# A row scale moved from the activations to the products, in two matmul stages of a transformer-block kernel

## The reference, cut to what matters

```
# first block's feed-forward (w_up is 1024 x 5632, 44 chunks of 128 outputs)
h = rmsnorm(x, norm_ffn_g) @ w_up          # rmsnorm: x * rsqrt(mean(x*x)) * g
h = causal_conv3(h, conv_w) + conv_b       # per channel, over tokens
a, b = split(h);  x = x + (silu(a) * b) @ w_down

# last layer's feed-forward (w1 is 1024 x 4096, 32 chunks)
h = rms(x, g) * (1 + scale) + shift
x = x + gate * square(relu(h @ w1)) @ w2
```

## Time and profile before

| | us |
|---|---|
| median of 3 runs | 1424.33 (1420.19 to 1426.97) |
| the profiled execution | 1423.98 |
| its span in the trace | 1422.2 |
| PE busy | 1366.4 (96%), 8436 matmuls |
| DVE busy | 714.1 (50%) |
| ACT busy | 604.7 (43%) |
| POOL busy | 448.6 (32%) |
| mean granted TensorE clock | 0.989 |

### The profile page before, as it was taken

How to read it: one execution, slowest core, us unless ns; L and a number is a source line. 1 busy time by engine, 2 the same in 40 slices (tenths; PEclk the granted TensorE clock), 3 DMA queues, 4 the chain that set the end, 5 groups by cost and what they waited for, 6 DMA issues and landing times.

```text
span 1422.2 us, 20872 instructions
## 1 busy us (share of the span) xinstructions
PE 1366.4 (96%) x8436; PEld 1158.2 (81%) x8436; DVE 714.1 (50%) x1129; ACT 604.7 (43%) x997; POOL 448.6 (32%) x440
## 2 busy tenths in 40 slices
PE   7889999999999999998999999999899999899999
PEld 7777788789999677875788888888577777799999
DVE  7575447757765635227122232222657766844443
ACT  6334445556664322225332133322445544665432
POOL 4532121333342000314440024401266643477200
PEclk9999999999999999999999999999999999999999
DMA  7346567686555445245533332323522221455552
GB/s 279 118 167 206 194 228 242 216 299 234 178 178 179 180 166 173 87 137 184 172 100 93 100 100 93 103 90 104 207 97 96 79 101 45 163 166 187 182 182 85
DMA packets 63968, 220.14 MB, mean 155 GB/s; under 512 B 6912, under 2 KB 10240, under 8 KB 63872
## 3 DMA queue, kind: packets, MB, share of 16 engines
q1 hardware_dynamic: 63584, 218.56, 46.2%
q10 hardware_dynamic: 288, 0.25, 0.1%
HBM read 217.73 MB, written 1.05 MB: 154 GB/s over the span
## 4 chain that ended last, share of the span: by engine, by line
PE 80%; DVE 9%; POOL 4%; ACT 3%; issue 2%; DMA 1%; SPq 0%; DVEq 0%; POOLq 0%; ACTq 0%
PE ps L476 23%; PE ps L490 22%; PE ps L488 22%; PE ps L532 3%; DVE wlo L1419 2%; PE ps L795 1%; POOL tmp L2144 1%; PE ps L822 1%; PE ps L742 1%; PE ps L809 1%; DVE tmp L1685 1%; DVE tmp L1687 1%; DVE Alo L1832 1%; PE ps L483 1%; PE ps L788 1%
## 5 line engine op out<-in xcount | busy, mean ns | idle before, releaser
L476 PE MATMUL ps<-Ahi,whi 128*128 128x256 f32 (+1 forms) x1656 | 552.6, 334 | 16.6 <-ACT Ahi L942 7.0
L490 PE MATMUL ps<-Ahi,wlo 128*128 128x256 f32 (+1 forms) x1584 | 509.2, 321 | 2.2 <-DVE wlo L1419 2.2
L488 PE MATMUL ps<-Alo,whi 128*128 128x256 f32 (+1 forms) x1584 | 509.4, 322 | 0.7 <-DVE Alo L1433 0.5
L1419 DVE TENSOR_TENSOR wlo<-raw,whi 128x1024 fp32r<-128x1024 f32 x298 | 373.3, 1261 | 226.6 <-ACT whi L913 226.5
L913 ACT ACTIVATE whi<-raw 128x1024 fp32r<-128x1024 f32 x305 | 320.2, 1052 | 263.9 <-PE ps L490 217.5
L476 PEld LDWEIGHTS ps<-Ahi,whi 128*128 128x128 f32 x1656 | 319.4, 193 | 93.8 <-issue 40.8
L490 PEld LDWEIGHTS ps<-Ahi,wlo 128*128 128x128 f32 x1584 | 305.2, 193 | 24.8 <-DVE wlo L1419 3.3
L488 PEld LDWEIGHTS ps<-Alo,whi 128*128 128x128 f32 x1584 | 305.4, 193 | 23.6 <-issue 1.9
L488 PE MATMUL ps<-Hlo,whi 128*128 128x256 f32 (+2 forms) x752 | 240.0, 319 | 0.4 <-DVE Hlo L1433 0.4
L476 PE MATMUL ps<-Hhi,whi 128*128 128x256 f32 (+2 forms) x712 | 229.0, 322 | 0.0
L490 PE MATMUL ps<-Hhi,wlo 128*128 128x256 f32 (+2 forms) x712 | 228.6, 321 | 0.0
(11 more groups left out here) (257 smaller groups left out, 1244.9 us busy)
## 6 DMA issues: line engine op xcount, KB each, us to landing
raw<-in_ada SPq DMA_DIRECT2D x96, 512.0 KB, 3.6
raw<-in_w SPq DMA_DIRECT2D x64, 512.0 KB, 3.5
raw<-in_w_up SPq DMA_DIRECT2D x44, 512.0 KB, 4.4
raw<-in_w_in SPq DMA_DIRECT2D x38, 512.0 KB, 4.5
raw<-in_w_0a SPq DMA_DIRECT2D x32, 512.0 KB, 3.5
raw<-in_w_0b SPq DMA_DIRECT2D x32, 512.0 KB, 3.5
raw<-in_na_in SPq DMA_DIRECT2D x24, 512.0 KB, 6.0
raw<-in_w_down SPq DMA_DIRECT2D x22, 512.0 KB, 3.5
```

The lines of the kernel that those rows point to most:

```text
L476: e.matmul(o, w_hi, ah, start=k == 0, stop=False)
L488: e.matmul(o, w_hi, al, start=False, stop=False)
L490: m = e.matmul(o, w_lo, ah, start=False, stop=last)
L1419: e.tensor_tensor(wlo[i % NRAW][:, :cols], raw[i % NRAW][:, :cols], plain(whi[s % NHI][:, :cols]), SUB).then_inc(S("wlo").sem, 1)
```

## The change

All 44 chunks of w_up and all 32 of w1_1 now take the activations without r, and DVE multiplies each product by r into `Y[n % 4]`. The normed activations of both stages, the special first chunk, and POOL's share of `wlo` in both go. A bank is free when DVE has multiplied, no longer when the convolution or the relu has read it. For w1_1 all 32 chunks have 258 columns, and `Ehi`, `Elo` lie in `Ahi`, `Alo` instead of in `Hhi`, `Hlo`. ACT reads `Y` instead of the bank (L1130, L1232), and so do DVE's L1685 and L1687.

```diff
-EARLY = {"w_in": 3, "w_up": 4, "w1_1": 3}
+EARLY = {"w_in": 3, "w_up": 44, "w1_1": 32}
...
-LOW_BY_POOL = [... ("w_in", 2), ("w_in", 3), ("w_up", 2), ("w_up", 3), ("w1_1", 2), ("w1_1", 3), ("w1_1", 4)]
+LOW_BY_POOL = [SPLIT_AT[key] for key in (("w_in", 2), ("w_in", 3))]
...
-    Ehi, Elo = [x[:, 8192 - 8 * 258:]... for x in (Hhi, Hlo)]
+    Ehi, Elo = [x.rearrange("p c t -> p (c t)")[:, :8 * 258]... for x in (Ahi, Alo)]
...
-        linear("w_up", 256, lambda k: (Ahi[:, k], Alo[:, k]), ready("n1_hi"), ready("n1_lo"), during=during_up,
-               following=..., first=(256, lambda k: (E_hi[:, k], E_lo[:, k]), ready("e1_hi"), ready("e1_lo")))
+        linear("w_up", 256, lambda k: (E_hi[:, k], E_lo[:, k]), ready("e1_hi"), ready("e1_lo"), during=during_up,
+               following=...)
...
-        linear("w1_1", 256, lambda k: (Ahi[:, k], Alo[:, k]), ready("m1_hi"), ready("m1_lo"), during=during_1,
-               first=(258, lambda k: (Ehi[:, k], Elo[:, k]), e2_hi, e2_lo))
+        linear("w1_1", 258, lambda k: (Ehi[:, k], Elo[:, k]), e2_hi, e2_lo, during=during_1)
... ACT, w_up, chunk n
                 if n == 0:
                     square_out(7)
                     root("n1", rst[:, LEFT])
-                    for c in range(3):
-                        normed_hi("n1", c, ...)
...
+                else:
                     up_finish(n - 1)
-                if n < 4:
-                    w.wait_ge(S("resc_w_up"), n + 1)
-                    o = Y[n][:, :256]
-                else:
-                    o = product("w_up", n)[:, :256]
+                w.wait_ge(S("resc_w_up"), n + 1)
+                o = Y[n % 4][:, :256]
... ACT, w1_1, chunk n
-                if n < 3:
-                    w.wait_ge(S("resc_w1_1"), n + 1)
-                    relu_up("r1", Y[n][:, :256], tmp[n % 5][:, :256], shift_out[:, n % 2:n % 2 + 1])
-                else:
-                    if n >= 5:
-                        w.wait_ge(S("h1_lo"), n - 4)
-                    relu_up("r1", product("w1_1", n)[:, :256], tmp[n % 5][:, :256])
+                w.wait_ge(S("resc_w1_1"), n + 1)
+                if n >= 5:
+                    w.wait_ge(S("h1_lo"), n - 4)
+                relu_up("r1", Y[n % 4][:, :256], tmp[n % 5][:, :256], shift_out[:, n % 2:n % 2 + 1])
... DVE, w_up, chunk n
-                if n < 4:
-                    rescaled("n1", "w_up", n, rst[:, LEFT])
-                    norm1_steps(*((0, 3), (3, 6), (6, 10), (0, 0))[n])
-                    w.wait_ge(S("resc_w_up"), n + 1)
-                    o = Y[n][:, :256]
-                else:
-                    o = product("w_up", n)[:, :256]
+                if n >= 4:
+                    w.wait_ge(S("up_conv"), n - 3)
+                rescaled("n1", "w_up", n, rst[:, LEFT])
+                w.wait_ge(S("resc_w_up"), n + 1)
+                o = Y[n % 4][:, :256]
... DVE, w1_1, chunk n
-                if n < 3:
-                    o = product("w1_1", n)
-                    if n == 2:
-                        w.wait_ge(S("r1"), 1)
-                    e.tensor_copy(shift_out[:, n % 2:n % 2 + 1], o[:, 256:257])...
-                    rescaled("m1", "w1_1", n, rst[:, LEFT])
-                    m1_steps(*((0, 4), (4, 10), (0, 0))[n])
+                o = product("w1_1", n)
+                if n >= 2:
+                    w.wait_ge(S("r1"), n - 1)
+                e.tensor_copy(shift_out[:, n % 2:n % 2 + 1], o[:, 256:257])...
+                rescaled("m1", "w1_1", n, rst[:, LEFT])
```

More of the change, by code:

```diff
@@ L151 @@
 HI_AT, LO_AT = split_places()
-LOW_BY_POOL = [SPLIT_AT[key] for key in (("w_in", 2), ("w_in", 3), ("w_up", 2), ("w_up", 3), ("w1_1", 2), ("w1_1", 3),
-                                         ("w1_1", 4))]
+LOW_BY_POOL = [SPLIT_AT[key] for key in (("w_in", 2), ("w_in", 3))]
 LOW = {s: ("wlo_p", LOW_BY_POOL.index(s) + 1) if s in LOW_BY_POOL else ("wlo", s + 1 - sum(p < s for p in LOW_BY_POOL))
@@ L345, in launch_program @@
     Olo = Hlo[:, 2048:4096].rearrange("p (c t) -> p c t", c=8)
-    Ehi, Elo = [x[:, 8192 - 8 * 258:].rearrange("p (c t) -> p c t", c=8) for x in (Hhi, Hlo)]
+    Ehi, Elo = [x.rearrange("p c t -> p (c t)")[:, :8 * 258].rearrange("p (c t) -> p c t", c=8) for x in (Ahi, Alo)]
     E_hi, E_lo = Ahi[:, :, RIGHT], Alo[:, :, RIGHT]
@@ L454, in linear @@
             kt, nt = WEIGHTS[name]
-            early = EARLY.get(name, 0)
+            early = EARLY.get(name, 0) if first else 0
             for n in range(begin, nt):
@@ L476, in linear @@
                     e.matmul(o, w_hi, ah, start=k == 0, stop=False)
-                    if kt == 8 and n == early:
+                    if kt == 8 and n == early and name not in ("w_up", "w1_1"):
                         low_ready(s)
@@ L692, in during_up @@
             written("w_up", n)
-        linear("w_up", 256, lambda k: (Ahi[:, k], Alo[:, k]), ready("n1_hi"), ready("n1_lo"), during=during_up,
-               following=lambda u: ada_following("w_up", u),
-               first=(256, lambda k: (E_hi[:, k], E_lo[:, k]), ready("e1_hi"), ready("e1_lo")))
+        linear("w_up", 256, lambda k: (E_hi[:, k], E_lo[:, k]), ready("e1_hi"), ready("e1_lo"), during=during_up,
+               following=lambda u: ada_following("w_up", u))
         def after_down(u):
@@ L1080, in scalar_program @@
                     after_out(7)
-        n1_x = [tmp[4], X[0], X[1]]
         def silu(m):
@@ L1107, in scalar_program @@
                     root("n1", rst[:, LEFT])
-                    for c in range(3):
[L1109 to L1113, removed]
-                if n == 2:
[L1115 to L1118, removed]
-                    up_finish(n - 1)
-                if n < 4:
-                    w.wait_ge(S("resc_w_up"), n + 1)
-                    o = Y[n][:, :256]
-                else:
-                    o = product("w_up", n)[:, :256]
+                else:
+                    up_finish(n - 1)
+                w.wait_ge(S("resc_w_up"), n + 1)
+                o = Y[n % 4][:, :256]
                 ch = n // 2 + 22 * (n % 2)
@@ L1373, in scalar_program @@
                     after_na_out(7)
[L1374 to L1379, removed]
         for what, i in walk("w1_1"):
@@ L1388, in scalar_program @@
                     root("m1", rst[:, LEFT])
[L1389 to L1395, removed]
-                    hidden_hi("h1", n - 1, 256)
-                if n < 3:
-                    w.wait_ge(S("resc_w1_1"), n + 1)
-                    relu_up("r1", Y[n][:, :256], tmp[n % 5][:, :256], shift_out[:, n % 2:n % 2 + 1])
-                else:
-                    if n >= 5:
-                        w.wait_ge(S("h1_lo"), n - 4)
-                    relu_up("r1", product("w1_1", n)[:, :256], tmp[n % 5][:, :256])
+                else:
+                    hidden_hi("h1", n - 1, 256)
+                w.wait_ge(S("resc_w1_1"), n + 1)
+                if n >= 5:
+                    w.wait_ge(S("h1_lo"), n - 4)
+                relu_up("r1", Y[n % 4][:, :256], tmp[n % 5][:, :256], shift_out[:, n % 2:n % 2 + 1])
         hidden_hi("h1", 31, 256)
@@ L1456, in rescaled @@
             w.wait_ge(S(st + "_r"), 1)
-            e.tensor_tensor(Y[n][:, :256], o[:, :256], r, MUL).then_inc(S("resc_" + name).sem, 1)
+            e.tensor_tensor(Y[n % 4][:, :256], o[:, :256], r, MUL).then_inc(S("resc_" + name).sem, 1)
         def ada_copied(quad):
@@ L1655, in vector_program @@
                 ada_place(i)
[L1658 to L1665, removed]
         for what, i in walk("w_up"):
@@ L2001, in vector_program @@
                     early_lo("e2", Ehi, Elo, 7, LEFT, G[:, 1, 1, 0, 7:8])
[L2002 to L2019, removed]
         for what, i in walk("w1_1"):
@@ L2027, in vector_program @@
                     mean_inverse("m1", rst[:, LEFT], ps[4][:, :256])
-                if n < 3:
-                    o = product("w1_1", n)
-                    if n == 2:
-                        w.wait_ge(S("r1"), 1)
-                    e.tensor_copy(shift_out[:, n % 2:n % 2 + 1], o[:, 256:257]).then_inc(own.sem, own.up())
-                    rescaled("m1", "w1_1", n, rst[:, LEFT])
-                    m1_steps(*((0, 4), (4, 10), (0, 0))[n])
+                o = product("w1_1", n)
+                if n >= 2:
+                    w.wait_ge(S("r1"), n - 1)
+                e.tensor_copy(shift_out[:, n % 2:n % 2 + 1], o[:, 256:257]).then_inc(own.sem, own.up())
+                rescaled("m1", "w1_1", n, rst[:, LEFT])
         for what, i in walk("w2_1"):
@@ L2135, in gpsimd_program @@
         parts("n1", ssum[:, :256], lambda c: sq[c % 2][:, :256])
-        low("w_up", 2)
-        low("w_up", 3)
         for c in range(22):
@@ L2230, in gpsimd_program @@
         parts("m1", ssum[:, :256], lambda c: sq[c % 2][:, :256])
-        for u in (2, 3, 4):
-            low("w1_1", u)
         hidden("h1", 32, 256, "r1")
```

2 lines of the change are left out of this document (1 added, 1 removed), and 6 rows, old and new, of the table IN_TURN.

## The result

The changed kernel takes 1430.88 us (median of six runs, 1429.45 to 1433.46), the kernel before 1423.55 in the same comparison: a ratio of 1.0051, interval 1.0032 to 1.0069. It is about half a per cent slower: the interval lies above 1, and the time at the upper end of what the prediction called no change (1417 to 1431). The forecast was 1428.0 with a range of 1414 to 1438. The profiled execution took 1429.88 us.

What follows compares the result with a forecast made beforehand. PE was taken as bound by its matmul rate but for waits and half clock at two starts, with a DVE-ACT-POOL ring close behind in w_up. w_up +11.7 and w1_1 -7.5 gave +4.2 us on 1423.98: 1428, range 1414 to 1438.

Steps and rivals of the forecast that it cites:

- w_up, start and first half: Waits and half clock at w_up's start go, -6.0 us; later `wlo` costs 0.9, longer laps in the first half 0.3.
- the cost of the later `wlo`: w_up's start: DVE now writes `wlo` of units 2 and 3 too, so PE waits, 0.9 us together.
- The 3.2 us counted for the half clock: w_up's start: 27 matmuls in 6.41 us at half clock would need 3.24 at full clock, saving 3.2 us.
- The ring in the second half: w_up: DVE, ACT and POOL wait on each other in a closed lap, 5.78 us for two chunks, growing to 6.98.
- The term of 16.5 us: w_up's second half and w_down's first three units: 13.5 pairs at 1.22 us each, +16.5 us.
- The step that failed: w_down: DVE has little to do there and PE runs at its own rate again, so no cost was counted.
- w1_1: Wait of 4.50 us and 3.1 us of half clock at its start go, -7.6; wider matmuls +0.1; together -7.5 us.
- The clock: w_up's second half: full clock and no cost, though PE will idle 1.22 of 6.98 us.
- A (no ring): Rival, w_up: the ring of engines is no bound, 1411 us, or 1417.6 with the multiply alone in it; chance 0.16.
- B (both halves): Rival, w_up: the even chunk's half is exposed too, lap 7.4 us, +5.4 and +3 us, 1436; chance 0.17.
- C: Rival: w1_1 gives nothing, PE waits for `wlo` of units 2 to 4 instead, up to 7.6 us, 1436; chance 0.10.
- D: Rival: the clock falls in w_up's second half for two or three stretches, partly won back, 1432; chance 0.05.

Runs made afterwards that it cites:

- w1_only: Kernel before the change, with the change made in w1_1 only and w_up left as it was; 1415.49 us, ratio 0.9958 to the kernel before.
- odd_no_trip: Changed kernel, but in w_up's odd chunks ACT's first tap reads the even chunk's product, so it needn't wait for the odd multiply; 1419.22 us.
- odd_twice: Changed kernel with one extra DVE multiply, into a place that isn't read, in each odd chunk of w_up from 5 on; 1437.83 us.
- even_twice: Changed kernel with one extra DVE multiply, into a place that isn't read, in each even chunk of w_up from 4 on; 1432.84 us.
- sum_later: Changed kernel, but PE does the row sum of the context's squares after w_down's sixth unit, not its fifth; 1425.41 us.
- up_only: Kernel before the change, with the change made in w_up only and w1_1 left as it was; 1440.28 us, ratio 1.013 to the kernel before.
- wlo_between: Changed kernel, but in every chunk of w_up DVE writes `wlo` between the multiply and the taps, not ahead of the multiply; 1412.18 us.

## Why the prediction was right, and where it was off

The time was off by 2.9 us, and the signs and order of the terms held. The near match owes something to errors that cancel: between the two traces w_up and w_down came out 3.5 us worse than forecast, w1_1 1.1 us better and the unchanged code 0.9 better. It owes something to luck too, since executions of one kernel differ by more than 2.9 us.

- *w_up, start and first half.* Forecast -6.0 + 0.9 + 0.3 = -4.8; measured -5.0. The ada pairs divide it. From the first pair to the second, where the old kernel has its waits and its half clock, 13.19 us became 7.07: -6.1, forecast -6.0. Ahead of that it is +0.4, the cost of the later `wlo`, forecast +0.9. Behind it PE takes 7.06 instead of 6.94 us from pair to pair, six times, since the lap is longer than forecast: +0.7, forecast +0.3. The 3.2 us counted for the half clock are no price of the clock by itself: `w1_only` shows that at full clock waits take most of its place, and 1.2 us are saved. All of it goes only because the normed activations go.
- *The ring in the second half.* The lap was forecast at 6.98 and is 7.07. The wait for L1112 at odd chunks is 0.74 us, as read from the earlier trace rows; PE's two delays in a lap are about 0.33 and 0.99 us, forecast a third and 0.9 (starts 0.35 and 1.00 us apart instead of 0.12, and 0.10 more until the next). `odd_no_trip`, `odd_twice` and `even_twice` bear it out half by half. The missing 0.09 is the even chunk's first tap, 0.57 instead of 0.48 us: it now reads `Y` from SBUF beside POOL's `Hlo`.
- *The term of 16.5 us.* Up to w_down's first matmul +14.4, forecast 12 x 1.22 = 14.6; 12 x 1.31 would be 15.7. The trace shows why 1.3 us less came out: PE isn't delayed at units 20, 21 and 23, and its first long delay is at unit 22 (326.74). So DVE did enter with a lead, where the prediction said that it had none. w_down's first three units are in the next +4.3; without the row sum's 2.2 they cost 2.1, and 14.4 + 2.1 = 16.5 is the term as forecast, a lap longer than forecast against a lead that wasn't.
- *The step that failed:* "In w_down DVE has little to do and PE runs at its own rate again." It asked only for `wlo`. PE has another supplier in w_down, POOL's sum of the context's squares, and ACT makes these squares only behind w_up's last `Hhi`. The earlier trace rows had the ring going through POOL and ACT; the step didn't ask what else waits in their queues. It cost 2.74 - 0.56 = 2.2 us of wait and, in this trace, 1.5 of half clock, 3.7 in all. `sum_later` shows both gone; `up_only` has the same wait without the half clock. With it w_up and w_down cost +15.2 where +11.7 was forecast.
- *w1_1.* Forecast -7.5, measured -8.6, with no wait for `wlo` of units 2 to 4. In the kernel before PE also waited for the remainder `Hlo` in w1_1's first chunk, 0.6 us with what follows, and this went too; the forecast didn't count it.
- *The clock.* The stretch from 340 to 398 stayed at 1.00 though PE lost 1.31 of each 7.07 us. The section weighed in the prediction (the Trainium skill, TensorE: Matmul & The Clock Gate, section "A second HAM failure mode: psum-queue depth-cycling") tells of another kernel whose clock swung when PE was idle for short times, but often. The granted clock in these rows doesn't swing.
- *The rivals.* A (no ring) is ruled out by the lap; B (both halves) by the lap and `even_twice`, though its ada copies do show in the four longer laps; C by w1_1's stretch; D by the clock in w_up.

Left open: the 0.7 us lost between w_down and w1_1, in unchanged code, and what decides about the clock behind the row sum. The 1.6 us ahead of w_up are no effect of the change that one could tell: over the thirteen traces w_up's row sum starts at anything from 251.08 to 256.46 us, behind the same code.

## What to carry to other kernels

A multiply moved into an in-order queue cost here by its place and by what stood behind it, 0.34 us a lap in one half and nothing in the other: draw the ring of engines for one lap, and put the added work where the ring already has idle time, or put other work into the round trip that it opens. When the engines of a ring get late, list everything that their queues feed later, also in the next stage. And try the parts apart: two large effects of opposite sign had made a change that looked like nothing.

## What the runs showed of the hardware

Of two overlapping instructions of DVE and POOL the later one was held up, and the one that started first wasn't. POOL's product takes 0.74 us when it starts first and 1.58 when `wlo` is 0.23 us ahead of it: it ends 0.59 us behind the end of `wlo` (346.10 + 1.22 = 347.32 to 347.91). When POOL is first, `wlo` takes 1.59 instead of 1.22. The even chunk's first tap joined in only with the change. In the kernel before it reads the product from the bank and took 0.48 us beside POOL's `Hlo`:

```profile
348.05 0.74 POOL L2048 TENSOR_TENSOR Hlo<-tmp,Hhi 128x256 fp32r<-128x256 f32 x1 [0.59 <-ACT Hhi L1093]
```

From `Y` it takes 0.57. In `wlo_between`, where `Hlo` is itself held by `wlo` and ends later (349.53), it takes 0.92. The Trainium skill (SBUF — State Buffer, section "Who interferes with whom") says that a VectorE instruction with two inputs in SBUF contends with a GpSimd instruction that reads SBUF, that one with at most one SBUF input doesn't (outside the two-port modes), and that the order of issue decides who is blocked. These rows agree with all three. The held one ends 0.59 us (POOL's product), 1.08 (`wlo`) and 0.28 (the tap) behind the end of the other, 0.14 to 0.20 less than it takes alone, so it isn't simply moved back as a whole.

Behind a wait of 2.74 us at the context's row sum the granted clock over the following 4 us or so was 0.57 in the changed kernel and in `odd_no_trip` and 0.65 in `even_twice`, but 1.00 in `up_only` and `odd_twice`, all with a wait of that length. At w_up's old start the same code had a mean of 0.83 from 256 to 276 us in the kernel before and 1.00 in `w1_only`. So one wait of this size sometimes brought PE to half clock and sometimes not; what decides isn't shown. Waits of 0.7 us in each 7.07 left it at full clock for 58 us.
